# Moving 512 projected features from the attention's fill-in work into a Strassen group behind the query and key products, with the heads' squares on VectorE

## The reference

```python
h = rms_norm(x, norm1_g)
proj = jnp.einsum('bsd,de->bse', h, w_in)             # 1024 x 1024 by 1024 x 6144
q, k, v, bg, cg, xc = jnp.split(proj, [...], axis=-1) # six times 1024 features
y_attn = chunked_relpos_attention(q, k, v, ...)       # begins with rms_norm of q and k per head of 64
y_conv = bg * conv(cg * xc)                           # depthwise, causal, width 3
gates = jax.nn.sigmoid(jnp.einsum('bsd,de->bse', h, w_gate) + b_gate)   # 2048 features
merged = g_attn * (y_attn @ w_attn_proj) + g_conv * (y_conv @ w_conv_proj)
x = x + merged @ w_out
```

## Time and profile before

| | us |
|---|---|
| median of three timed executions | 2191.71 (2190.46 to 2192.29) |
| the profiled execution | 2192.57 |
| its span in the trace | 2190.8 |
| TensorE matmul busy | 2154.3 (98%) |
| VectorE busy | 1474.2 (67%) |
| ScalarE busy | 948.5 (43%) |
| GpSimd busy | 984.0 (45%) |

### The profile page before, as it was taken

One profiled execution on the slowest core, in us unless ns is written; L12 is line 12 of the kernel. 1 busy time (PEld: TensorE's weight loads), 2 busy tenths in 40 slices (PEclk: granted clock), 3 DMA queues, 4 the chain that ended last, 5 costly groups with the idle time before them and its releaser, 6 DMA issues.

```text
span 2190.8 us, 29144 instructions
## 1 busy us (share of the span) xinstructions
PE 2154.3 (98%) x10474; PEld 1797.2 (82%) x10474; DVE 1474.2 (67%) x2591; ACT 948.5 (43%) x1694; POOL 984.0 (45%) x707
## 2 busy tenths in 40 slices
PE   9999999999888999999999999999999999999999
PEld 8888888888767888888888888888878888788887
DVE  6776765368584666666666483332777786898886
ACT  5555425343424555555555221211555545433332
POOL 3233465535443322313132264547465655656564
PEclk9999999999999999999999999999999999999999
DMA  6320124323134333323232473224134445826433
GB/s 229 104 75 20 45 110 154 133 103 116 58 125 121 108 88 92 87 87 110 66 110 68 154 252 129 92 71 179 62 115 163 163 150 188 314 94 233 150 125 114
DMA packets 200382, 271.43 MB, mean 124 GB/s; under 512 B 58248, under 2 KB 118440, under 8 KB 200016
## 3 DMA queue, kind: packets, MB, share of 16 engines
q1 hardware_dynamic: 123968, 200.33, 26.8%
q10 hardware_dynamic: 76304, 69.64, 10.3%
HBM read 192.28 MB, written 86.05 MB: 127 GB/s over the span
## 4 chain that ended last, share of the span: by engine, by line
PE 83%; DVE 8%; ACT 3%; issue 3%; POOL 2%; DMA 1%; ACTq 0%; DVEq 0%; SPq 0%; POOLq 0%
PE ps L203 71%; PE ps L2170 3%; PE ps L2157 2%; PE ps L2145 2%; DVE res L1985 1%; PE ps L778 1%; DVE res L2003 1%; DVE qkv_raw L1974 1%; PE ps L753 1%; PE ps L764 1%; DVE qkv_head_stat L1992 1%; DVE k_lo L2390 1%; POOL w_lo L3028 1%; PE ps L2182 1%; DVE pt_lo L2438 0%
## 5 line engine op out<-in xcount | busy, mean ns | idle before, releaser
L158 POOL TENSOR_TENSOR w_hi<-w_raw,zero 128x512 fp32r<-128x512 f32 x184 | 209.9, 1171 | 784.5 <-PE ps L203 660.3
L203 PE MATMUL ps<-a_hi,w_hi 128*128 128x512 f32 x1408 | 544.6, 407 | 8.3 <-DVE res L1985 7.5
L203 PE MATMUL ps<-a_hi,w_lo 128*128 128x512 f32 x1408 | 524.3, 393 | 0.0
L203 PE MATMUL ps<-a_lo,w_hi 128*128 128x512 f32 x1408 | 521.9, 391 | 0.0
L203 PE MATMUL ps<-w_hi,a_hi 128*128 128x512 f32 (+1 forms) x960 | 369.9, 385 | 9.5 <-POOL w_lo L1830 5.7
L203 PE MATMUL ps<-w_hi,a_lo 128*128 128x512 f32 (+1 forms) x960 | 368.1, 383 | 0.0
L203 PE MATMUL ps<-w_lo,a_hi 128*128 128x512 f32 (+1 forms) x960 | 367.7, 383 | 0.0
L203 PEld LDWEIGHTS ps<-a_hi,w_lo 128*128 128x128 f32 x1408 | 265.0, 188 | 59.0
L203 PEld LDWEIGHTS ps<-a_hi,w_hi 128*128 128x128 f32 x1408 | 265.6, 189 | 51.7 <-issue 9.5
L203 PEld LDWEIGHTS ps<-a_lo,w_hi 128*128 128x128 f32 x1408 | 266.3, 189 | 42.1
L163 POOL TENSOR_TENSOR w_lo<-w_raw,w_hi 128x512 fp32r<-128x512 f32 x184 | 255.1, 1417 | 3.6
(11 more groups left out here) (295 smaller groups left out, 3851.7 us busy)
## 6 DMA issues: line engine op xcount, KB each, us to landing
w_raw<-in_w_in_dram SPq DMA_DIRECT2D x26, 1024.0 KB, 5.3
mlp_part<-u_parts SPq DMA_DIRECT2D x26, 1024.0 KB, 8.0
feat_fm<-stage ACTq DMA_DIRECT2D x68, 256.0 KB, 2.1
u_parts<-mlp_acc SPq DMA_DIRECT2D x28, 512.0 KB, 2.8
u_parts<-res SPq DMA_DIRECT2D x28, 512.0 KB, 2.8
conv_in<-feat_fm ACTq DMA_DIRECT2D x24, 512.0 KB, 5.8
res<-in_x_dram SPq DMA_DIRECT2D x16, 512.0 KB, 6.4
w_raw<-in_w_out_dram SPq DMA_DIRECT2D x8, 1024.0 KB, 5.1
```

The costliest lines, as they stand in the source:

```text
L158: hi = nc.gpsimd.tensor_tensor(w_hi[slot][:, k:k + 2, :], w_raw[:, k:k + 2, :], zero[:, 0:1].unsqueeze(2).to_broadcast([P, 2, CW]), ALU.add)
L203: last = nc.tensor.matmul(out_of(o), lhs, rhs(o), start=first and n == 0, stop=final and n == 2)
```

## The change

Four things are changed. (1) The first 512 features of bg are taken out of the chunks (`BCX_GROUPS = 1`) and computed in `phase_qkv` behind k, as seven more Strassen products s = 14 to 20 of 24 matmuls each. Their weights are the stationary side, each engine has its own steps for them, and ScalarE's and VectorE's take two banks at a time (`copy_group`, `add_group`). (2) The attention still takes 17 chunks, now 10 and 7 gate chunks, so the merging stage has one gate chunk (2 units) left instead of three; `conv(1)` to `conv(7)` move behind VectorE's multiplication in units v = 0 to 6, and their loads into ScalarE's loop over v. (3) `weight_sum` of the next unit's m5 and m2 is done one product earlier (after m1's and m7's additions). (4) The heads' squares are done by VectorE, directly ahead of the sum per head; ScalarE keeps the root.

```diff
-        W_BCX2 = seg(io["w_in_2"], 0, 3072, 12)
+        BCX_GROUPS = 1
+        W_BCX2 = seg(io["w_in_2"], 0, 3072 + 512 * BCX_GROUPS, 12 - 2 * BCX_GROUPS)
...
-            GATES = 6
+            GATES = 2 * (W_AP - start)
...
                     for w in range(GATES - 1):
                         gate_out(w)
-                        if w < 4:
-                            conv_load(w + 2)
...
-                        if v == 1:
-                            conv_load(7)
+                        if v < 6:
+                            conv_load(v + 2)
...
-                    for f in range(6):
-                        conv(f)
+                    conv(0)
                     for k in range(KB):
                         low(0, k)
-                    conv(6)
...
-                        if v == 2:
-                            conv(7)
+                        if v < 7:
+                            conv(v + 1)
...
+                    for s in range(NS, NP):
+                        p, before = ORDER[s % 7], user_before(s, bank_pair)
+                        pe.wait_ge(*low_w.at(s + 1))
...
+                        for fb in range(2):
+                            cols = slice(fb * P, (fb + 1) * P)
+                            for k in range(4):
+                                last = three_passes(lambda _: ps[:, 2 * bank_pair(s) + fb, :], wh[:, k, cols], wl[:, k, cols],
+                                                    lambda _: high[:, k, :], lambda _: low[:, k, :], (0,), k == 0, k == 3)
+                        last.then_inc(mm_b.sem, 1)
+                    pe.wait_ge(*plain_lo.at(2))
...
+                    def copy_group(s):
+                        act.wait_ge(*mm_b.at(s - NS + 1))
+                        for r, c, sign in COPIED[ORDER[s % 7]]:
+                            last = nc.scalar.activation(acc((s - NS) // 7, r)[:, 2 * c:2 * c + 2, :],
+                                                        ps[:, 2 * bank_pair(s):2 * bank_pair(s) + 2, :], ACT.Copy, scale=sign)
+                        last.then_inc(b_copied.sem, 1)
...
-                    def squares(s):
+                    def roots(s):
                         u, c = s // 7, WHOLE[ORDER[s % 7]]
-                        act.wait_ge(*added.at(added_to(s, 3)))
-                        nc.scalar.activation(spare[:, :, :], quarter(*c), ACT.Square).then_inc(q_sq.sem, 1)
                         act.wait_ge(*q_red.at(4 * u + DONE_ORDER.index(c) + 1))
...
-                        if s + 2 < NS:
-                            weight_high(s + 2)
+                        weight_high(s + 2)
...
                         if p in WHOLE:
-                            squares(s)
+                            roots(s)
+                    for s in range(NS, NP):
+                        p, g = ORDER[s % 7], (s - NS) // 7
...
+                        if p in COPIED:
+                            copy_group(s)
+                        if s + 2 < NP:
+                            weight_high(s + 2)
+                        if s == G_LAST + 1:
+                            first_high()
...
                     def norm_heads(s):
                         u, c = s // 7, WHOLE[ORDER[s % 7]]
                         n = 4 * u + DONE_ORDER.index(c) + 1
+                        for store in v_store:
+                            dve.wait_ge(*store.at(32))
+                        dve.wait_ge(*added.at(added_to(s, 3)))
+                        nc.vector.tensor_tensor(spare[:, :, :], quarter(*c), quarter(*c), ALU.mult).then_inc(q_sq.sem, 1)
                         dve.wait_ge(*q_sq.at(n))
...
-                        ahead = {1: 3, 2: 3, 3: 3, 5: 2, 6: 2}.get(s % 7)
-                        if ahead is not None and s + ahead < NS:
-                            weight_sum(s + ahead)
+                        if 1 <= s % 7 <= 5:
+                            weight_sum(s + 3)
                         if p in WHOLE:
                             norm_heads(s)
...
+                    for s in range(NS, NP):
+                        if ORDER[s % 7] in ADDED:
+                            add_group(s)
+                        if 1 <= s % 7 <= 5 and s + 3 < NP:
+                            weight_sum(s + 3)
```

More of the change, by code:

```diff
@@ L338, in unit, with free_banks @@
                         last.then_inc(done, 1)
[L340 to L341 removed]
+                    def free_banks(w):
+                        if w < 4:
+                            for read in banks_read[w]:
+                                pe.wait_ge(*read)
+                        elif w < GATES + 4:
                             pe.wait_ge(ev_gate, w - 3)
                         else:
[L344 to L345 removed]
+                            pe.wait_ge(ev_fm, u0 + w - GATES + 1)
+                    for w in range(GATES):
+                        free_banks(w)
                         unit(w, mm_gate, None, w == GATES - 1)
                     for v in range(16):
[L348 to L351 removed]
+                        free_banks(GATES + v)
                         unit(GATES + v, mm_fm, lo0 + v if v % 8 == 0 else None, v % 8 == 7)
@@ L1820, in _ @@
-                        store_quarter(u, (1, 1))
+                            next_loads(2)
+                        store_quarter(u, (1, 0))
+                        sp.wait_ge(*low_w.at(s0 + 7))
+                        if more:
+                            sp.dma_start(rc, rows_of(u + 1, 0, 1)).then_inc(c_load.sem, 16)
+                        else:
+                            next_loads(3)
+                        store_quarter(u, (0, 0))
+                        store_quarter(u, (1, 1))
+                    for g in range(NG):
+                        last = g == NG - 1
+                        sp.wait_ge(*low_w.at(last_of(g, "m7")))
+                        if last:
+                            sp.wait_ge(*spare_in.at(16))
+                            sp.dma_start(spare[:, :, :], spare_x[1]).then_inc(spare_in.sem, 16)
+                            load_weights(sp, W_BCX2 + 1, W_BCX2 + 2)
+                        elif g + 2 < NG:
+                            sp.wait_ge(*left_in.at(16 * (g + 2)))
+                            load_group(g + 2, 0)
+                        else:
+                            load_first()
+                        sp.wait_ge(*low_w.at(last_of(g, "m6")))
+                        if not last and g + 2 < NG:
+                            sp.wait_ge(*right_in.at(16 * (g + 2)))
+                            load_group(g + 2, 1)
+                        elif not last:
+                            sp.dma_start(rc, spare_x[0]).then_inc(spare_in.sem, 16)
+                        for r in range(2):
+                            sp.wait_ge(*b_added.at(5 * g + 4 + r))
+                            rows = feat2[512 * g:512 * (g + 1), 512 * r:512 * (r + 1)].rearrange("(f p) n -> p f n", p=P)
+                            if g:
+                                sp.wait_ge(*b_store[r].at(16 * g))
+                            sp.dma_start(rows, acc(g, r)).then_inc(b_store[r].sem, 16)
@@ L1852, in _ @@
                         high, low = operand(p)
[L1853 removed]
+                        wh, wl = weight(w_hi, s), weight(w_lo, s)
                         for t in range(4):
@@ L1865, in _ @@
                             last.then_inc(mm_q.sem, 1)
-                    pe.wait_ge(plain_lo, 2)
+                    for s in range(NS, NP):
+                        p, before = ORDER[s % 7], user_before(s, bank_pair)
+                        pe.wait_ge(*low_w.at(s + 1))
+                        if before is None:
+                            pe.wait_ge(*added.at(added_to(NS - 2 + bank_pair(s) // 2, 1 + 2 * (bank_pair(s) % 2))))
+                        elif ORDER[before % 7] in COPIED:
+                            pe.wait_ge(*b_copied.at(2 * ((before - NS) // 7) + before % 7 + 1))
+                        else:
+                            pe.wait_ge(*b_added.at(added_b(before)))
+                        high, low = operand(p)
+                        wh, wl = weight(w_hi, s), weight(w_lo, s)
+                        for fb in range(2):
[5 more added lines that the diff above has]
+                    pe.wait_ge(*plain_lo.at(2))
                 @block.scalar
@@ L1875, in weight_high @@
                     def weight_high(s):
-                        p = ORDER[s % 7]
-                        if s >= 2:
+                        p, u = ORDER[s % 7], s // 7
+                        if 2 <= s < NS:
                             act.wait_ge(*mm_q.at(4 * (s - 1)))
+                        elif s >= NS:
+                            before = user_before(s, place)
+                            if before is None:
+                                act.wait_ge(*mm_q.at(4 * (NS - 1 + place(s) // 2)))
+                            else:
+                                act.wait_ge(*mm_b.at(before - NS + 1))
                         if p in SUMMED:
@@ L1975, in weight_sum, with add_group @@
                         last.then_inc(w_sum.sem, 1)
```

(10 more changed lines are left out.)

161 lines of the change are left out of this document (108 added, 53 removed).

## The result

| | before | after |
|---|---|---|
| median of the timed executions, us | 2191.99 (2190.46 to 2192.29, 4 executions) | 2206.26 (2203.41 to 2210.57, 4) |
| the profiled execution | 2192.57 | 2203.41 |
| its span | 2190.8 | 2201.6 |

The ratio is 1.0068, with a 95% interval of 1.0053 to 1.0083: the change makes the kernel slower by 14 us. The prediction was 2202.5 us, slower. The profiled execution of after is the fastest of its four, so its trace, which shows +10.8 us, has about 3 us less to explain than the medians.

The account below looks back on a forecast made before the run. TensorE, busy 98% of the span, was taken as the bound, losing 25.4 us in the query and key stage. 2192.6 - 43.5 + 53.9 + 0.5 = 2203.5; being 0.9 above the median, 2202.5 us, own range 2197 to 2208.

Parts of the forecast that it names:

- Gate units: Merging stage: four units of 48 matmuls, 10.88 us each, leave it, worth -43.5 us.
- the merging stage's waits: At v = 7, low parts run against TensorE's use of them: 0 to 6 us, taken as 0.5.
- The merging rival: Merging stage bound by VectorE too, low parts at v = 7 in full collision: +6, 2209 us; chance 0.14.
- The chain of q: VectorE's steps from m4's additions to m3's root at 539.3, then a 7.4 us stall before m6 and 1.9 half clock.
- the rival that VectorE keeps up: Multiplications escape GpSimd's collisions, m3's root of q before about 534, no stall before m6: 2186 us; chance 0.14.
- k's m5, m2 and m4: TensorE stalls in k: 1.2 us before m5, 2.9 before m2, 5.0 before m4 with 1.8 of clock.
- A full collision of the multiplications: VectorE's four multiplications beside GpSimd take 6.8 instead of 2.5 us; sign: 6 to 7 us in most places.
- The other sign: Profile after: TensorE idle 3 to 5 us before k's m4.
- k's m6 and the group's m4: TensorE stalls: 7.4 us plus 1.9 of clock before k's m6, 9.2 plus 1.8 before the group's m4.
- The wait for the attention's load: TensorE's wait of 6.21 us for the attention's first load shrinks to some 0.3, with no half clock behind.
- The sum: Up to the attention: stalls and clock 40.8 against 25.4 us before, so +15.4; with +38.6 of matmuls, +54.0.
- The rival that the early sums pay in full: Waits before k's m5 and m2 and at the load go, none replaces them: -16.2, 2171.5 us; chance 0.05.

Follow-up runs that it names:

- The third experiment: The changed kernel, with GpSimd starting the low part of m7 only when VectorE has normed m4's quarter: 2202.91 us, ratio 1.0042.
- the first: The changed kernel with the heads' squares back on ScalarE, all else as changed: 2180.91 us, ratio 0.9953.
- the fourth experiment: The changed kernel, with ScalarE copying the high parts of the group's m4 and m3 ahead of the root of k's m6: 2202.98 us, ratio 1.0046.

## Why the prediction was right, by its steps

**Gate units.** Predicted -43.5 and +0.5 for the merging stage's waits, -43.0 together; measured -41.9 from the attention's last wait to the MLP's first matmul. The two short waits for low parts of the convolution's operands cost 1.6 us instead of 0.5. The merging rival (+6) is out.

**The chain of q.** Predicted and measured: square of m4 done 516.3 and 515.9; small steps 520.4 and 520.1; multiplications 527.2 and 527.0; root of m3 539.3 and 538.9; low part of m6 started 540.3 and 539.9; m6 started 548.8 and 548.4, after a wait of 7.4 and 7.25. The step that decided, that the multiplications begin just as GpSimd does, came true with 0.2 us between them. The third experiment took that collision alone away and got 3.9 of the 7.25 us back, and the first took the square away and got all. That is shown. With the root at 538.9 and not before 534, the rival that VectorE keeps up is out. Not tested is ScalarE's order at m6: no run put m6's high part ahead of m3's root. VectorE's additions end last there, and how much earlier they would come with GpSimd's group moved ahead is open.

**k's m5, m2 and m4.** Here single terms were off and cancelled. m5 waited 2.02 instead of 1.2 us, and half clock came behind it, which the prediction left out. That made TensorE itself later (at m2 at 577.0, not 574.0), and VectorE came to the additions that free its bank at 574.2, not 576.3, so m2 did not wait at all (2.9 predicted). m4 waited 2.67 instead of 5.0: the root of m6 was done at 581.8, not 583.7. This lead of 1.9 us was there at the root of m7 already (566.0 for 567.9), and most of it comes from m2's weight sum: done at 560.0, not 561.7, since it took 3.55 us where about 4.4 were charged. m5's low part took 9.09 us beside this sum and the square, where about 7.2 were charged, and was done at 564.5 for 563.1. These are the terms that were mis-sized. GpSimd's, VectorE's and ScalarE's timeline of after:

```profile
555.38 9.09 POOL L1920 TENSOR_TENSOR w_lo<-qkv_raw,w_hi 128x512 fp32r<-128x512 f32 x4 [10.04 <-ACT w_hi L2004]
```

```profile
556.46 3.55 DVE L2123 TENSOR_TENSOR qkv_raw<-qkv_raw 128x1024 f32<-128x1024 f32 x2
```

```profile
565.68 0.32 ACT L2030 ACTIVATE qkv_head_stat<-qkv_head_stat,eps_t 128x32 f32<-128x32 f32 x1 [9.43 <-DVE qkv_head_stat L2156]
```

A full collision of the multiplications was charged wherever GpSimd works beside them, and the sign of it was to be 6 to 7 us in most places. Only q's m4 has that (6.82); five others take 4.55 to 4.67, and two run alone in 2.50. In four of the five GpSimd's first pieces meet the small steps instead, as m3's above (1.29 and 1.19), so that the chain from root to last multiplication loses 4.2 us all the same. The other sign that did not come is k's m4: 2.67 us, not 3 to 5.

**k's m6 and the group's m4.** 8.31 for 7.4, starting at 645.2 for 646.2; 8.97 for 9.2, starting at 678.6 for 679.5. The order on ScalarE was the reason given for the second, and the fourth experiment shows it. The wait for the attention's load shrank from 6.21 to under 0.3 us, as predicted: 719.59, the first of its matmuls, shows none, and the 0.49 at 720.74 is for ScalarE.

**The sum.** By waits and clock: predicted 40.8 (33.4 of waits, 7.4 of clock), measured about 40 (29.7 and 10). The clock was sized too small, the waits too large, and that the two cancel is luck. The attention's first matmul came at 719.6 for 720.2. The profiled executions differ by +10.8 for +10.9 predicted: +54.1 up to the attention's last wait for +53.9, -41.9 in the merging stage for -43.0, and -1.4 in the MLP, for which the prediction had nothing. The path and the long waits are as predicted; that the total agrees within 0.1 is luck. Of the 3.8 us that the median lies above the forecast, the trace, itself of a run at 2203.41, shows none. The rival that the early sums pay in full (-16.2) is out as well: they are worth 2.6 us in the kernel before.

**What varies between runs.** One wait in the MLP, far behind the change, differs between profiled executions: TensorE waits for a low part, and ahead of it VectorE waits for a DMA of `u_parts`. VectorE's row of after and the same place in the kernel in which GpSimd waits (a line number two higher), one fence for each:

```profile
1862.51 3.50 DVE L3434 TENSOR_TENSOR res<-res 128x1024 f32<-128x1024 f32 x3 [1.89 <-DMA u_parts<-res]
```

```profile
1861.61 3.50 DVE L3436 TENSOR_TENSOR res<-res 128x1024 f32<-128x1024 f32 x3 [9.76 <-DMA u_parts<-res]
```

TensorE's wait there is 0.34 us in the first and 4.14 us in the second; in before it is 1.70 (VectorE's 4.11) and with the squares on ScalarE 3.00 (6.51). Over all ten traces it is 0.53 to 1.70 us in the three kernels without the group, 2.82 to 4.14 in the six experiments with it, and 0.34 in after. So after's trace, of its fastest run, is the odd one among the kernels with the group; with a wait like theirs it would be some 3 us longer, about what the median lies above it. Whether the DMA lands later or the work around it comes sooner, these points don't tell. It fits a part of the spread of 7 us within after's four runs, but no trace of a longer one of them was taken, and that stays open.

**The rules weighed.** The port rule of the Trainium skill (page "SBUF — State Buffer", section "Who interferes with whom": two SBUF inputs on VectorE and a GpSimd read exclude each other for the whole instruction) now has rows at 2048 elements. GpSimd's group beside two sums and the square took 9.11 us where beside the sums alone it took 7.07, and the square waited 1.1. The trace agrees. The same section says that the order of issue decides who blocks; the square in four pieces fits it, with 2.4 us lost by VectorE and 1.2 won by GpSimd, but no run here changed the order of issue alone.

## What to carry to other kernels

Moving a short step from an idle engine to a busy one costs what stands behind it in both orders: here 2.3 us per square on VectorE (3.4 beside GpSimd), eight times, became 22 to 25 us, because the longer chain pushed multiplications or small steps into GpSimd's next group, freed PSUM banks late, and held ScalarE's weights behind a late root. Price such a move by following the chain to the next instruction that another engine starts by its own clock. When several edits come together, time the largest suspect alone in both directions: three of the four edits here won 11 us together, and the fourth hid it.
